# A hybrid decoder layer on one core: the output projection as three fp32r products instead of one fp32 product

## The reference

```python
z = rmsnorm(x) @ w_in                      # 544 rows x 1024, w_in 1024 x 1536
a_out = pool_mix(z[:, :512])               # four window means, per-group linear map, scale
v = head_layernorm(gelu(z[:, 1024:]))
b_out = gelu(z[:, 512:1024]) * (sgu_w @ v + sgu_b)       # per head and chunk of 128 positions
x = x + concat([a_out, b_out]) @ w_out     # the output projection, 1024 x 1024
h = rmsnorm(x)
logits = h @ w_router + b_router           # top 4 of 32 experts, softmax of the four
x = x + sum_k weight_k * expert_k(h)       # clamped SwiGLU, w_up 1024 x 2048, w_down 1024 x 1024
x = x + sigmoid(x @ w_ple_gate) * (p @ w_ple_proj)
y = rmsnorm(x)
```

## Time and profile before

| | |
|---|---|
| median of 3 timed runs | 1441.78 us (1441.73 to 1443.72) |
| time of the profiled execution | 1444.58 us |
| its span, first to last instruction | 1442.8 us |
| mean granted TensorE clock | 0.99 of full |
| busy: PE, DVE, ACT, POOL | 1410.2, 1233.2, 928.4, 218.9 us |

### The profile page before, as it was taken

The page is one execution under the profiler, slowest core; times in us unless marked ns, Lnnn a source line. Parts: engine busy times, 40 slices in busy tenths (PEclk is TensorE's granted clock), DMA queues, the critical chain, the costliest instruction groups (busy, mean ns, idle before and its releaser), DMA issues.

```text
span 1442.8 us, 19410 instructions
## 1 busy us (share of the span) xinstructions
PE 1410.2 (98%) x6551; PEld 1134.8 (79%) x6551; DVE 1233.2 (85%) x1007; ACT 928.4 (64%) x629; POOL 218.9 (15%) x130
## 2 busy tenths in 40 slices
PE   7999999999999999999999999999999999999997
PEld 5895557888888888888888888888888888888665
DVE  5742458999999999999999999999999999999885
ACT  4311236767777777777777777777777777777622
POOL 3131000221111111111111111111111111111100
...
DMA packets 94169, 457.32 MB, mean 317 GB/s; under 512 B 13314, under 2 KB 14894, under 8 KB 60213
## 3 DMA queue, kind: packets, MB, share of 16 engines
...
q10 hardware_dynamic: 526, 1.60, 0.4%
...
## 4 chain that ended last, share of the span: by engine, by line
PE 94%; DVE 2%; issue 1%; ACT 1%; DMA 1%; POOL 0%; POOLq 0%; DVEq 0%; ACTq 0%
PE ps L1296 48%; PE ps L1305 24%; PE ps L1164 5%; PE ps L1445 2%; PE ps L1312 2%; PE ps L1284 2%; PE ps L1277 2%; PE ps L1099 1%; PE ps L1101 1%; PE ps L1106 1%; DVE resid L1935 1%; PE ps L1246 1%; PE ps L1044 1%; PE ps L1187 1%; PE ps L1041 1%
## 5 line engine op out<-in xcount | busy, mean ns | idle before, releaser
L1707 DVE TENSOR_TENSOR w_lo<-raw,w_hi 128x2048 fp32r<-128x2048 f32 x384 | 868.2, 2287 | 58.9 <-PE ps L1305 58.3
L878 ACT ACTIVATE w_hi<-raw 128x2048 fp32r<-128x2048 f32 x384 | 732.2, 1916 | 212.3 <-PE ps L1296 171.7
L1296 PE MATMUL ps<-w_hi,xT_hi 128*128 128x512 f32 x1024 | 278.4, 394 | 1.2 <-ACT xT_hi L897 1.1
L1296 PE MATMUL ps<-w_hi,xT_lo 128*128 128x512 f32 x1024 | 275.2, 391 | 0.1
L1305 PE MATMUL ps<-w_lo,xT_hi 128*128 128x512 f32 x1024 | 274.7, 390 | 0.0
L1296 PEld LDWEIGHTS ps<-w_hi,xT_lo 128*128 128x128 f32 x1024 | 192.6, 188 | 41.8 <-DVE xT_lo L1763 0.5
L1305 PEld LDWEIGHTS ps<-w_lo,xT_hi 128*128 128x128 f32 x1024 | 192.8, 188 | 40.3
L1296 PEld LDWEIGHTS ps<-w_hi,xT_hi 128*128 128x128 f32 x1024 | 190.4, 189 | 40.1 <-ACT xT_hi L897 1.4
L729 POOL DMA_INDIRECT expert_rows<-y_rows,scatter_col x32 | 145.6, 4551 | 402.8 <-ACT y_rows L911 402.8
L1296 PE MATMUL ps<-w_hi,aT_hi 128*128 128x512 f32 x512 | 139.9, 395 | 0.0
L1296 PE MATMUL ps<-w_hi,aT_lo 128*128 128x512 f32 x512 | 136.9, 389 | 0.0
...
...
## 6 DMA issues: line engine op xcount, KB each, us to landing
raw<-in_w_up_dram SPq DMA_DIRECT2D x256, 1024.0 KB, 6.5
raw<-in_w_down_dram SPq DMA_DIRECT2D x128, 1024.0 KB, 7.5
raw<-in_w_ple_gate_dram SPq DMA_DIRECT2D x4, 1024.0 KB, 5.4
yk<-expert_rows SPq DMA_DIRECT2D x4, 1024.0 KB, 7.0
raw<-expert_rows SPq DMA_DIRECT2D x4, 1024.0 KB, 6.5
...
w_v_sb<-in_w_in_dram SPq DMA_DIRECT2D x2, 1024.0 KB, 8.2
w_z_sb<-in_w_in_dram SPq DMA_DIRECT2D x2, 1024.0 KB, 13.1
```

The source lines that it names most:

```text
L878: act.activation(w_hi[:, s % SPLIT, :], raw[:, s % RING, :], ACT.Copy).then_inc(s_hi, 1)
L1296: mm = pe.matmul(out[:, c:c + 512], (xh, xl)[xs], w_hi[:, s % SPLIT, base + c:base + c + 512], start=(fresh and xs == 0 and base == 0), st ...
L1707: dve.tensor_tensor(w_lo[:, s % SPLIT, :], raw[:, s % RING, :], w_hi[:, s % SPLIT, :].bitcast(F32), ALU.subtract).then_inc(s_lo, 1)
```

## The change

The output projection becomes three fp32r products. `w_out` is split into high parts (`w_out_hi0`, `w_out_hi1`, `w_out_hi23`, `w_out_hi_b`) on ACT and low parts (`w_out_lo_a`, `w_out_lo_b`) on DVE, in five pieces counted by `s_woh` and `s_wol`. DVE writes the mixed rows rounded to fp32r into `ext_hi` and `uT_hi`, which lie over `ext` and `uT`, and what is left into `mix_lo`. Tiles 0 and 1 are taken together in the first half of the row blocks (blocks 0 and 1, then 2 and 3). The last gating product and its sum are done before the last u product. The bias table is split before tile 0 is added. The split parts of `w_out` lie over all six slots of `raw`, so chunks 4 and 5 of the first expert are no longer loaded before; chunk s now goes to slot (s + 2) mod 6, and chunks 0 and 1 wait for `s_outa` (the first half of the last tile), 2 to 5 for the last product. `xn2` and `h2T` have one buffer each. What follows is the core of the diff.

```diff
-        for g in range(G):
+        for g in range(LASTG):
             JOBS += [(("u", g), "A"), (("pool", g), "V"), (("gating", g), "V")]
+        JOBS += [(("gating", LASTG), "V"), (("u", LASTG), "A"), (("pool", LASTG), "V")]
...
+        def slot(s):
+            return (s + 2) % RING
+
+        def w_out_part(k):
+            return (1, 2, 3, 3, 4, 4, 5, 5)[k]
+
+        def w_out_hi(k):
+            return (w_out_hi0[:], w_out_hi1[:], w_out_hi23[:, 0], w_out_hi23[:, 1])[k] if k < KD // 2 else w_out_hi_b[:, k - KD // 2]
+
+        def w_out_lo(k):
+            return (w_out_lo_a, w_out_lo_b)[k // (KD // 2)][:, k % (KD // 2)]
+
+        def mix_low(k):
+            return mix_lo[:, k] if k < KD - 1 else mix_lo7[:]
...
-                    if s in (RING - 2, RING - 1):
-                        sp.wait_ge(s_job, JOB[("u", G - 1)] + 1)
+                    if s < 2:
+                        sp.wait_ge(s_outa, 1)
...
-            for c in range(RING - 2, RING):
-                load_up(0, c, 0, c)
-
             sp.wait_ge(s_mix, 2 * G)
-            sp.wait_ge(s_out, 16 * STORES)
+            sp.wait_ge(s_out, 16)
             for t in range(TT):
                 if t == LAST - 1:
-                    sp.wait_ge(s_bias, 4)
                     load(p_sb[:, 0:LAST, :], p_prompt[0, 0].rearrange("(t p) n -> p t n", p=P), "p")
                     load(p_sb[0:NS, LAST, :], p_sample.rearrange("a b s n -> (a b s) n"), "p")
+                if t == LAST:
+                    sp.wait_ge(s_outa, 1)
                     load(w_proj_sb[:], w_ple_proj.rearrange("a (k p) n -> p (a k) n", p=P), "ple")
-                if t == LAST:
-                    load_up(0, 0, 0, 0)
-                    load_up(0, 1, 0, 1)
+                    for c in range(4):
+                        load_up(0, c, 0, c)
                 sp.wait_ge(s_xn, TT + t + 1)
-                sp.dma_start(xn_dram[t * P:t * P + NT[t], :], xn[0:NT[t], t % 2, :]).then_inc(s_xrow[t], 16)
-            for c in (*range(2, RING - 2), *range(RING, UP_CHUNKS)):
+                sp.dma_start(xn_dram[t * P:t * P + NT[t], :], xn2[0:NT[t], :]).then_inc(s_xrow[t], 16)
+            for c in range(4, UP_CHUNKS):
...
+                if g == LASTG:
+                    act.wait_ge(ld["w_out"], 16)
+                    act.wait_ge(s_pout, 16 * POOL_STORES)
+                    act.activation(w_out_hi0[:], w_out_a[:, 0], ACT.Copy).then_inc(s_woh, 1)
+                    act.activation(w_out_hi1[:], w_out_a[:, 1], ACT.Copy).then_inc(s_woh, 1)
...
+            act.activation(w_out_hi23[:], w_out_a[:, 2:4], ACT.Copy).then_inc(s_woh, 1)
             act.wait_ge(s_mix, 2 * G)
-            act.wait_ge(s_out, 16 * STORES)
+            act.wait_ge(s_out, 16)
             for i in range(2):
                 act.dma_start(bias_raw[i * E:(i + 1) * E, 0:2 * FF], b_up[0]).then_inc(ld["bias"], 16)
             for i in range(3):
                 act.dma_start(bias_raw[i * E:(i + 1) * E, 2 * FF:], b_down[0]).then_inc(ld["bias"], 16)
+            for i in range(2):
+                act.wait_ge(ld[("w_out2", "w_out3")[i]], 16)
+                act.activation(w_out_hi_b[:, 2 * i:2 * i + 2], w_out_b[:, 2 * i:2 * i + 2], ACT.Copy).then_inc(s_woh, 1)
...
+            bias_high()
             for t in range(TT):
                 square2(t)
-                if t == 1:
-                    bias_high()
-                if t >= 2:
-                    act.wait_ge(s_lgp, t - 1)
+                if t >= 1:
+                    act.wait_ge(s_lgp, t)
                 act.wait_ge(s_h2p, t + 1)
-                act.activation(h2T[:, t % 2, :, :], h2_banks.rearrange("p a (b n) -> p (a b) n", n=P),
-                               ACT.Copy).then_inc(s_h2d, 1)
+                act.activation(h2T[:], h2_banks.rearrange("p a (b n) -> p (a b) n", n=P), ACT.Copy).then_inc(s_h2d, 1)
...
+            for g in range(G):
+                project(("u", g), lambda k: w_u_hi[:, k], w_u_lo, g)
+                pool_products(g)
+                if g < LASTG:
+                    gating_products(g)
+                if g == LASTG - 1:
+                    gating_products(LASTG)
...
-            def out_part(i, half, b):
+            def out_part(i, ks, part):
                 n = NT[i]
-                if half == 0 and b == 0:
-                    if i < 2:
-                        pe.wait_ge(s_emptied["V"], EMPTIED[("gating", G - 2 + i)])
+                first = part == 0 and ks[0] == 0
+                last = part == 2 and ks[-1] == KD - 1
+                if first:
+                    if i == 0:
+                        pe.wait_ge(s_emptied["V"], EMPTIED[("gating", G - 2)])
+                    elif i == 1:
+                        pe.wait_ge(s_emptied["V"], EMPTIED[("pool", LASTG)])
                     else:
                         pe.wait_ge(s_outd, i - 1)
-                for k in range(w_z_halves[half].start, w_z_halves[half].stop):
-                    if i == 0 and b == 0:
-
-                        pe.wait_ge(s_mix, 2 * G - 1 if k < KD - 1 else 2 * G)
-                        if k == KD // 2:
-                            pe.wait_ge(ld["w_out2"], 16)
-                        if k == 3 * KD // 4:
-                            pe.wait_ge(ld["w_out3"], 16)
-                    rows_k = ext[:, k, LEAD + i * P:LEAD + i * P + n] if k < G else uT[:, k - G, i * P:i * P + n]
-                    w = (w_out_a, w_out_b)[half][:, k % (KD // 2), b * 512:(b + 1) * 512]
-                    mm = pe.matmul(out_banks(i)[0:n, b, :], rows_k, w, start=(k == 0), stop=(k == KD - 1),
-                                   skip_group_check=True)
-                if half == 1 and b == 1:
+                if i == 0:
+                    if part == 0:
+                        pe.wait_ge(s_woh, w_out_part(ks[-1]))
+                        pe.wait_ge(s_mix, (2 * (G - 1) if ks[-1] < LASTG else 2 * G - 1) if ks[-1] < G else 2 * G)
+                    elif part == 1:
+                        if ks[-1] < G:
+                            pe.wait_ge(s_emptied["V"], EMPTIED[("pool", ks[-1])])
+                        else:
+                            pe.wait_ge(s_mixlo, G)
+                    else:
+                        pe.wait_ge(s_wol, w_out_part(ks[-1]))
+                for b in range(2):
+                    for k in ks:
+                        cols = slice(i * P, i * P + n)
+                        if part == 1:
+                            rows_k = mix_low(k)[:, cols]
+                        else:
+                            rows_k = ext_hi[:, k, LEAD + i * P:LEAD + i * P + n] if k < G else uT_hi[:, k - G, cols]
+                        w = w_out_lo(k) if part == 2 else w_out_hi(k)
+                        mm = pe.matmul(out_banks(i)[0:n, b, :], rows_k, w[:, b * 512:(b + 1) * 512], start=(first and k == 0),
+                                       stop=(last and k == KD - 1), skip_group_check=True)
+                if last:
                     mm.then_inc(s_outp, 1)
+                elif i == LAST and part == 2:
+                    mm.then_inc(s_outa, 1)
...
+            halves = (range(0, KD // 2), range(KD // 2, KD))
+            for ks in (range(0, 2), range(2, KD // 2)):
+                for part in range(3):
+                    for i in range(2):
+                        out_part(i, ks, part)
+            for part in range(3):
+                out_part(0, halves[1], part)
+            out_part(1, halves[1], 0)
+            h2_transposes(0)
+            out_part(1, halves[1], 1)
+            router(0)
+            out_part(1, halves[1], 2)
+            for i in range(2, TT):
+                out_part(i, halves[0], 0)
+                if i == 2:
+                    ranks(0)
+                out_part(i, halves[0], 1)
+                h2_transposes(i - 1)
+                out_part(i, halves[0], 2)
+                out_part(i, halves[1], 0)
+                router(i - 1)
+                out_part(i, halves[1], 1)
+                out_part(i, halves[1], 2)
+                ranks(i - 1)
...
-                dve.tensor_scalar(ext[:, g, LEAD:LEAD + SEQ], bank(name), scaleT[:, g:g + 1], None, ALU.mult).then_inc(s_mix, 1)
-                dve.tensor_scalar(ext[:, g, LEAD + SEQ:LEAD + T], bank(name, 1)[:, 0:NS], scaleT[:, g:g + 1], None,
-                                  ALU.mult).then_inc(s_emptied["V"], 1)
+                dve.tensor_scalar(ext_hi[:, g, LEAD:LEAD + SEQ], bank(name), scaleT[:, g:g + 1], None, ALU.mult)
+                dve.tensor_scalar(ext_hi[:, g, LEAD + SEQ:LEAD + T], bank(name, 1)[:, 0:NS], scaleT[:, g:g + 1], None,
+                                  ALU.mult).then_inc(s_mix, 1)
+                dve.wait_ge(s_mix, 2 * g + 1)
+                dve.scalar_tensor_tensor(out=mix_lo[:, g, 0:SEQ], in0=bank(name), scalar=scaleT[:, g:g + 1],
+                                         in1=ext_hi[:, g, LEAD:LEAD + SEQ].bitcast(F32), op0=ALU.mult, op1=ALU.subtract)
```

(38 more changed lines are left out.)

118 lines of the change are left out of this document (64 added, 54 removed).

## The result

The changed kernel took 1433.01 us (median of 4, 1430.52 to 1433.71), the kernel before, timed beside it, 1442.74 us (median of 4): ratio 0.9932, 95% interval 0.9919 to 0.9944, 9.7 us faster. The forecast was 1429.0, with a range of its own from 1427.0 to 1431.0: the median lies 2.0 us above that range and at the very end of the range for 8 in 10 (1433.0). Timed side by side again in the experiments, unchanged, the two kernels lay 9.7 (a_again) and 10.1 us (a_third) apart. Over all experiments the kernel before has 37 timed runs with a median of 1442.40 us (1439.08 to 1444.70) and the changed one 16 with 1433.01 us (1429.63 to 1435.65), 9.4 us apart; drawing both sets anew many times gives 8.3 to 12.1 us. The profiled pair lie 14.1 us apart, 1444.58 and 1430.52 us (span 1428.7): the first is among the slowest executions of its kernel, the second among the fastest.

A forecast was written before the change was run, and what follows sets the result against it. PE's chain was taken to bound the kernel, the projection by its own products. From 1441.78 us, products -13.7 and a first wait of +0.9 give 1429.0 us; own range 1427.0 to 1431.0, 8 in 10 1426.0 to 1433.0.

The forecast's parts named there:

- The products: Output projection on PE: 80 fp32 products (69.5 us) become 240 fp32r products at 0.2325 us (55.8 us), gaining 13.7 us.
- The first wait: Projection start: after four products PE waits 0.9 us (bounds 0 to 1.3) for DVE's mix_lo to free the banks.
- Deliveries by DVE and ACT: Weight parts and mixed rows that DVE and ACT prepare for the projection arrive before PE asks: all hidden, no cost.
- The bias table: Split before tile 0's residual sum: lands about 122 us, tile 0 ready for PE at 129.7, hidden with 1.5 us spare.
- Moved without cost: Single buffers for h2T and normed rows, and later loads of the first expert's chunks, cost nothing; 6.5 us if cover failed.
- The sum: Whole kernel: products -13.7 plus first wait +0.9 gives -12.8 us, from 1441.78 to 1429.0 us.
- The experts' pace: Rival: projection products run as fast as the experts' products, 54.3 us instead of 55.8; kernel 1427.5 us; chance 0.12.
- a late table: Rival: PE waits up to 5.3 us for the bias table at the first transposes; kernel 1430 to 1435.8 us; chance 0.16.
- a give-back at the first expert: Rival: first expert's chunks that lost their early load arrive late, costing 6.5 us; kernel 1435.5 us; chance 0.04.
- a low clock in the projection: Rival: clock stays low through the projection, kernel slower by over 0.2%, up to 1484.8 us; chance 0.03.
- everything behind it moves with it: After the projection: all later work shifts earlier by the projection's full 12.8 us, giving 1429.0 us.

The follow-up runs named there:

- a_again: The changed kernel timed and profiled once more, nothing altered: 1433.81 us, ratio 0.9934 to the kernel before.
- a_third: The changed kernel, unaltered, timed again beside the versions padded with empty PE instructions, for a third profile: 1431.66 us.
- fewer_low: Against the changed kernel, 56 of 240 projection products left out, keeping only the last row block of each low-weight part: 1420.39 us, ratio 0.9849 to the kernel before.

## Why the prediction was right, and where it was off

- **The products.** Right: 1.86 us for eight, 0.2325 each, at full clock. The Trainium skill, "TensorE: Matmul & The Clock Gate", section "Back-to-back issue gap", has 215.7 ns for an isolated product of this width. No profile here shows that pace; the fastest is the experts', 0.907 us for four or 0.227 each.
- **The first wait.** Right: 0.93 us against 0.9, for the instruction that was named. The timeline behind it runs 0.3 us ahead of the forecast throughout, but only since the projection began at 111.04 us and not at 111.65: from its first product to the one behind the wait it took 2.11 us instead of the 1.85 of the forecast, since the four products ahead of the wait last 1.18 us with the drain of their last one, and not 0.93. With 1.18 instead of 0.9 us for the wait the sum gives 12.5 us.
- **Deliveries by DVE and ACT.** Right: nothing was late. The rounding copy took 0.63 us instead of 0.45, within its bounds.
- **The bias table.** Right: landed at 122.5 us, and tile 0's sum was done at 129.25 + 1.29 = 130.54 us, 0.4 before PE came to its transposes; fewer_low shows the wait that appears when 3.3 us of products go. The margin was thinner than the 1.5 us of the forecast: DVE was through with the table at 128.9 us and not at 128.4, PE came 0.3 us earlier, and the last product of tile 0, which my line left out, set the start of the sum 0.3 us behind the table.
- **Moved without cost.** Right: ACT makes the high parts of chunks 2 to 5 without a wait for DMA, and PE waits for no chunk up to chunk 8.
- **The sum.** The projection gained 80.77 - 68.17 = 12.60 us against 12.8 predicted, in each of the three profiles of the changed kernel.
- **The rivals.** The experts' pace, a late table, a give-back at the first expert and a low clock in the projection all stayed out.

What failed is the last step of the sum, "everything behind it moves with it". Of 12.6 us the medians keep 9.4 to 10.1. The 28 steps between moved exactly (991.2 us in each profile). Shown to be lost behind them: 0.5 to 0.9 us in the last step, by the place of the code. Argued from profiles only: the longer low stretch near 1365 us, with the rest at 100.9 us or more instead of 99.4 to 100.1, came in five of eight profiles with a shift of 160 and in none of six with another; the mean rest is 100.5 us in the eight and 99.9 in the six, so it would be 0.6 us on average. What is left, 1 to 2 us, goes with how often the clock is low: the timed runs have a mean granted clock of 0.9922 before (33 runs with a record) and 0.9897 after (16). Time times clock is 1431.2 and 1418.0 us, 13.2 apart, so at full clock the gain would be there, as it nearly is between runs of like clock (12.0 us, under a_again); but this product counts half of every low microsecond as lost, also where PE waits anyway, and is a rough measure. Why the changed kernel spends more time low stays open: only profiled runs show the places, and theirs are the same for both kernels.

My forecast of 1429.0 also took the median of three runs as base, 1441.78; it is 1442.4 over 37. Off that base the same sum gives 1429.6, so 0.6 of the 4.0 us between forecast and median come from the base.
